# The last norm's turn to token rows: moved into the last product phase, with the deviation applied to rows and eight half-row stores

## What is computed

```python
def odd_block_end(x, mix, l1_w_out_2, final_norm_gain_2):
    x = x + mix @ l1_w_out_2                 # (512, 2048) @ (2048, 2048)
    xf = x.astype(jnp.float32)
    y = xf * lax.rsqrt(jnp.mean(xf * xf, axis=-1, keepdims=True) + 1e-6)
    return y * final_norm_gain_2             # out: (1, 512, 2048)
```

## Time and profile before

| | us |
|---|---|
| median of three executions | 3452.27 |
| lowest, highest | 3450.07, 3458.89 |
| profiled execution | 3455.26 |
| its span in the trace | 3453.5 |
| TensorE busy | 3346.3 (97%) |
| VectorE, ScalarE, GpSimd busy | 1637.2, 1289.0, 520.9 |

### The profile page before, as it was taken

One profiled execution on the slowest core, in us unless ns is written; L12 is line 12 of the kernel. 1 busy time (PEld: TensorE's weight loads), 2 busy tenths in 40 slices (PEclk: granted clock), 3 DMA queues, 4 the chain that ended last, 5 costly groups with the idle time before them and its releaser, 6 DMA issues.

```text
span 3453.5 us, 41721 instructions
## 1 busy us (share of the span) xinstructions
PE 3346.3 (97%) x16417; PEld 2702.4 (78%) x16417; DVE 1637.2 (47%) x2691; ACT 1289.0 (37%) x1997; POOL 520.9 (15%) x754
## 2 busy tenths in 40 slices
PE   7999999999999999999999899999999999999996
PEld 6777887888888888888887676788878788777885
DVE  7895654434344444344344655543324333455532
ACT  4443433343233333433342445433223333456322
POOL 0001312323110000100331010121000111110211
PEclk9999999999999999999999999999999999999998
DMA  6776433546348776544335343453434733433631
GB/s 208 217 234 195 129 104 111 157 141 215 121 169 218 220 216 171 183 146 145 119 108 177 107 132 105 143 193 119 146 85 130 217 120 107 138 116 107 215 129 68
DMA packets 278948, 525.06 MB, mean 152 GB/s; under 512 B 64126, under 2 KB 99525, under 8 KB 273633
## 3 DMA queue, kind: packets, MB, share of 16 engines
q1 hardware_dynamic: 222352, 336.59, 32.6%
q0 software_dynamic: 54224, 182.52, 15.5%
q10 hardware_dynamic: 2176, 3.28, 0.4%
HBM read 408.32 MB, written 113.97 MB: 151 GB/s over the span
## 4 chain that ended last, share of the span: by engine, by line
PE 70%; DVE 4%; ACT 3%; DMA 2%; issue 2%; POOL 1%; ACTq 0%; DVEq 0%; POOLq 0%
PE pg L603 61%; PE pm L1288 2%; PE pm L1317 2%; DMA mx_g<-zt 2%; PE pm L1304 1%; PE pm L2392 1%; ACT whi L386 1%; PE pm L2396 0%; PE pm L2380 0%; DVE r_y L1673 0%; DVE d_x L2480 0%; ACT stage L481 0%; DVE xa L699 0%; ACT w_p L1353 0%; POOL mx_o L850 0%
## 5 line engine op out<-in xcount | busy, mean ns | idle before, releaser
L392 DVE TENSOR_TENSOR wlo<-raw,whi 128x1024 fp32r<-128x1024 f32 x523 | 664.3, 1275 | 1253.9 <-ACT whi L386 1253.0
L386 ACT ACTIVATE whi<-raw 128x1024 fp32r<-128x1024 f32 x523 | 548.6, 1054 | 1103.7 <-PE pg L603 1103.2
L603 PE MATMUL pg<-a_hi,whi 128*128 128x512 f32 x1856 | 744.3, 401 | 11.6 <-DVE wlo L392 4.3
L603 PE MATMUL pg<-a_hi,wlo 128*128 128x512 f32 x1856 | 727.2, 392 | 0.0
L603 PE MATMUL pg<-a_lo,whi 128*128 128x512 f32 x1856 | 726.4, 391 | 0.0
L603 PE MATMUL pg<-b_hi,whi 128*128 128x512 f32 x1568 | 618.9, 395 | 8.9 <-DVE stage L546 3.2
L603 PE MATMUL pg<-b_hi,wlo 128*128 128x512 f32 x1568 | 611.5, 390 | 0.0
L603 PE MATMUL pg<-b_lo,whi 128*128 128x512 f32 x1568 | 611.0, 390 | 0.0
L603 PEld LDWEIGHTS pg<-a_hi,whi 128*128 128x128 f32 x1856 | 348.5, 188 | 91.0 <-issue 14.3
L603 PEld LDWEIGHTS pg<-a_hi,wlo 128*128 128x128 f32 x1856 | 348.3, 188 | 77.9
L603 PEld LDWEIGHTS pg<-a_lo,whi 128*128 128x128 f32 x1856 | 348.9, 188 | 73.6 <-issue 2.6
(11 more groups left out here) (434 smaller groups left out, 3844.8 us busy)
## 6 DMA issues: line engine op xcount, KB each, us to landing
raw<-in_l_w_in SPq DMA_DIRECT2D x169, 512.0 KB, 3.7
raw<-in_ab_w_in SPq DMA_DIRECT2D x112, 512.0 KB, 3.7
zt<-stage POOLq DMA_DIRECT2D x142, 256.0 KB, 3.6
raw<-in_c_w_in SPq DMA_DIRECT2D x64, 512.0 KB, 5.0
raw<-in_l_w_out SPq DMA_DIRECT2D x64, 512.0 KB, 3.7
raw<-in_ab_w_out SPq DMA_DIRECT2D x32, 512.0 KB, 3.7
raw<-in_glu_w SPq DMA_DIRECT2D x32, 512.0 KB, 4.4
raw<-in_c_w_out SPq DMA_DIRECT2D x32, 512.0 KB, 3.7
```

The costliest lines, as they stand in the source:

```text
L386: nc.scalar.activation(used(whi, n), used(raw, n), ACT.Copy).then_inc(hi_ready, 1)
L392: nc.vector.tensor_tensor(used(wlo, n), used(raw, n), used(whi, n).bitcast(F32), ALU.subtract).then_inc(lo_ready, 1)
L603: ins = nc.tensor.matmul(pg[m][:r.rows(m), :r.cols()], lhsT, rhs, start=(kt == 0 and n_pass == 0), stop=(kt == r.kts - 1 and n_pass == 2))
```

## The change

The turning to rows no longer waits for the deviation. A row's deviation is one number per token, so it can be applied after the turn, as a factor per partition.

- In `act_piece` each residual tile of the last phase is also multiplied by its gain into one of four slots (`WEIGHT_SLOTS`: two of `xa_n`, `xa_acc`, `xa_r`), right behind its square.
- `token_rows_pe` transposes the four squares of such a tile into one bank of `pm0` to `pm2`; `token_rows_dve` copies the bank back over the tile in `xa`. For tiles 0 to 11 that is done inside the second to fourth block: the group of tile 4(i-1)+q-2 stands between the two halves of piece q (2 to 5) on TensorE, the copy at piece q+1 on VectorE.
- GpSimd adds 15 squares. The 16th goes to the sum directly: `finish_pe` sums per 128 tokens into one column each, from `acc` and from `xa_sq`, so that the sum stands as tokens by partition (`rstd_col`). Tile 15 is transposed behind the sums.
- The table for Ln and Exp is loaded once, in the second block at piece 2.
- `finish_act` and `finish_dve` multiply the rows of 128 tokens by their deviation into `y_tok`, half a row (1024 features) each; `y_tok` lies over `b_hi` and `b_lo`, so both wait for the last product. `finish_sp` issues eight stores of 512 KB on SyncE's queue and waits for them.

```diff
+    Y = overlay(HALF, [("y_tok", [NTOK, D], F32)])
+    TURNED = 4 * NTOK + 1
+    WEIGHTED = 5 * KT
+    WEIGHT_SLOTS = [XA["xa_n"][:, 0, :], XA["xa_n"][:, 1, :], XA["xa_acc"][:, :], XA["xa_r"][:, :]]
...
+    def token_rows_pe(pe, n):
+        pe.wait_ge(nh_ready, WEIGHTED + n + 1)
+        if n >= 3:
+            pe.wait_ge(xt_ev, TURNED + n - 2)
+        for t in range(NTOK):
+            ins = nc.tensor.transpose(pm[n % 3][:, t * P:(t + 1) * P], WEIGHT_SLOTS[n % 4][:, t * P:(t + 1) * P], ident[:, :])
+        ins.then_inc(xt_ready, 1)
+    def token_rows_dve(dve, n):
+        dve.wait_ge(xt_ready, TURNED + n + 1)
+        nc.vector.tensor_copy(XA["xa"][:, n, :], pm[n % 3][:, :]).then_inc(xt_ev, 1)
     def act_piece(act, r, i, q, extra, part):
         if part == 0:
...
         if extra["joint"] is not None and r is extra["first"] and i == 0 and q == 2:
+        if extra["last"] and i == 1 and q == 2:
+            nc.scalar.preload_act_table_set(LOG_EXP)
         if extra["gain"] is not None and i == r.blocks - 1 and 0 < q < r.pieces - 1:
             for kt in (2 * q - 2, 2 * q - 1):
...
                 if extra["gain"] is not None and i == r.blocks - 1:
+                if extra["last"]:
+                    if n >= 4:
+                        act.wait_ge(xt_ready, TURNED + n - 3)
+                    nc.scalar.activation(WEIGHT_SLOTS[n % 4], x[:, n, :], ACT.Copy, scale=col("last_g", n)).then_inc(nh_ready, 1)
         elif r.evac == "glu":
             for m in range(r.banks):
...
+        if extra["last"] and i and 3 <= q <= 6:
+            token_rows_dve(dve, MT * (i - 1) + q - 3)
         if extra["gain"] is not None and i == r.blocks - 1 and q > 1:
             for kt in (2 * q - 4, 2 * q - 3):
...
+        if extra["last"] and i and part == 1 and 2 <= q <= 5:
+            token_rows_pe(pe, MT * (i - 1) + q - 2)
         if joint is not None and r is extra["first"] and i == 0 and part == 0:
             if q == 3:
...
         elif r.evac == "resid":
             _, _, sq, sq_gained = X_OF["B" if extra["src"] == "A" else "A"]
             sums = [(acc, sq)] + ([(XA["xa_acc"], sq_gained)] if extra["two"] else [])
-            for m in range(r.banks):
+            for m in range(r.banks - 1 if extra["last"] and i == r.blocks - 1 else r.banks):
                 for s, (total, squares) in enumerate(sums):
...
-    def rstd_pe(pe):
-        pe.wait_ge(acc_done, 6 * KT)
-        nc.tensor.matmul(pm[0][:, :], ones[:, :], acc[:, :], start=True, stop=True).then_inc(rs_ready, 1)
-    def rstd_act(act):
+    def finish_pe(pe):
+        for n in range(KT - MT, KT - 1):
+            token_rows_pe(pe, n)
+        pe.wait_ge(acc_done, 6 * KT - 1)
+        pe.wait_ge(sq_ready, 5 * KT)
+        for t in range(NTOK):
+            nc.tensor.matmul(pm[3][:, t:t + 1], acc[:, t * P:(t + 1) * P], ones[:, 0:1], start=True, stop=False)
+            ins = nc.tensor.matmul(pm[3][:, t:t + 1], XA["xa_sq"][:, (KT - 1) % 2, t * P:(t + 1) * P], ones[:, 0:1], start=False, stop=True)
+        ins.then_inc(rs_ready, 1)
+        token_rows_pe(pe, KT - 1)
+    def rows_of_half(t, h):
+        return (Y["y_tok"][:, t, h * D // 2:(h + 1) * D // 2].rearrange("p (k c) -> p k c", c=P),
+                XA["xa"][:, h * KT // 2:(h + 1) * KT // 2, t * P:(t + 1) * P])
+    def finish_act(act):
-        serial(act, act_seq)(nc.scalar.activation(rstd[:, :], pm[0][:, :], ACT.Ln, scale=1.0 / D, bias=eps[:, 0:1]))
-        nc.scalar.activation(rstd[:, :], rstd[:, :], ACT.Exp, scale=-0.5).then_inc(sd_ready, 1)
-    def rstd_dve(dve):
+        serial(act, act_seq)(nc.scalar.activation(rstd_col[:, :], pm[3][:, :NTOK], ACT.Ln, scale=1.0 / D, bias=eps[:, 0:1]))
+        nc.scalar.activation(rstd_col[:, :], rstd_col[:, :], ACT.Exp, scale=-0.5).then_inc(sd_ready, 1)
+        act.wait_ge(sd_ready, 9)
+        act.wait_ge(w_used, pieces_in_all)
+        act.wait_ge(xt_ev, TURNED + KT // 2)
+        for t in range(NTOK):
+            y, x = rows_of_half(t, 0)
+            nc.scalar.activation(y, x, ACT.Copy, scale=rstd_col[:, t:t + 1]).then_inc(nh_ready, 1)
+    def finish_dve(dve):
+        for n in range(KT - MT, KT):
+            token_rows_dve(dve, n)
+        dve.wait_ge(w_used, pieces_in_all)
+        dve.wait_ge(xt_ev, TURNED + KT)
+        for t in range(NTOK):
+            y, x = rows_of_half(t, 1)
+            nc.vector.tensor_scalar(y, x, rstd_col[:, t:t + 1], None, ALU.mult).then_inc(xn_ready, 1)
+    rows_out = ident_in
+    def finish_sp(sp):
+        for t in range(NTOK):
+            for h, (signal, n) in enumerate(((nh_ready, WEIGHTED + KT), (xn_ready, 2 * KT))):
+                sp.wait_ge(signal, n + t + 1)
+                half_row = slice(h * D // 2, (h + 1) * D // 2)
+                sp.dma_start(out[0, t * P:(t + 1) * P, half_row], Y["y_tok"][:, t, half_row]).then_inc(rows_out, 16)
+        sp.wait_ge(rows_out, 16 + 16 * 2 * NTOK)
     def split_norm_dve(dve, x, xn, gain, hi, lo):
```

More of the change, by code:

```diff
@@ L173, in build @@
     r_sp = sb("r_sp", [6, RB])
-    ident_in = sem("identity_in")
+    ident_in = sem("identity_in_and_rows_out")
     NCONST = len(VECTORS) + 3
@@ L695, in split_norm_act @@
             nc.scalar.activation(hi[:, kt, :], xn[:, kt % 2, :], ACT.Copy).then_inc(nh_ready, 1)
[L697 to L700, removed]
     tokens_moved = [sem(f"token_rows_moved{n}") for n in range(NTOK)]
@@ L779, in turn_in_dve @@
         run(vec.tensor_copy(rstd[:, :], pm[0][:, :]))
[L782 to L806, removed]
     def store_x(pool, x, n):
@@ L2559, in details @@
     def details(n):
-        d = dict(ready=None, old=None, acc0=0, xin0=0, gain=None, done=0, two=False, joint=JOINTS.get(n))
+        d = dict(last=(n == L1_OUT), ready=None, old=None, acc0=0, xin0=0, gain=None, done=0, two=False, joint=JOINTS.get(n))
         d.update(DETAILS.get(n, {}))
@@ L2639, in _ @@
             in_turn(products(sp, n, sp_piece))
+        finish_sp(sp)
     @block.gpsimd
@@ L2665, in _ @@
         mixed(mix_pool(pool, 2, ZT["mgate"], L1_GATES, 1), rest, pool, pool_piece, L1_OUT)
-        turn_out_pool(pool, XB["xb_tok"])
     @block.tensor
@@ L2689, in _ @@
         mixed(mix_pe(pe), rest, pe, pe_piece, L1_OUT)
-        rstd_pe(pe)
-        turn_out_pe(pe, XA["xa"])
+        finish_pe(pe)
     @block.scalar
@@ L2718, in _ @@
         mixed(mix_act(act, 2), rest, act, act_piece, L1_OUT)
-        rstd_act(act)
-        turn_out_act(act, XB["xb_tok"])
+        finish_act(act)
     @block.vector
@@ L2752, in _ @@
         mixed(mix_dve(dve, 2, B["b_lo"]), rest, dve, dve_piece, L1_OUT)
-        rstd_dve(dve)
-        scale_x_dve(dve, XA["xa"], "last_g")
+        finish_dve(dve)
     ctx.close()
```

## The result

| | before | after |
|---|---|---|
| median, us | 3452.26 (4 executions) | 3432.66 (4 executions) |
| lowest, highest | 3450.07, 3458.89 | 3431.25, 3434.74 |
| profiled execution | 3455.26 | 3432.28 |
| its span | 3453.5 | 3430.5 |

The ratio is 0.9943, with an interval of 0.9931 to 0.9955: the change takes off 0.57%, 19.6 us, where 19.2 was forecast.

The account below looks back on a forecast made before the run. TensorE bounds the kernel up to the last matmul, then a chain no product covers. Earlier last landing -19.1, transposes among the products +5.7, shorter landing to end -5.8: -19.2, so 3433.1 us; range 3427 to 3440.

Follow-up runs that it names:

- the version with mixed stores: The version with all transposes behind, but with five stores: first 128 rows in two halves, the other three groups whole (1 MB); 3427.05 us, ratio 0.9931.
- the version with all transposes behind: Changed kernel with all sixteen transpose groups behind the last product, none inside the product phase; 3427.16 us, ratio 0.9930; measured again 3427.77, 0.9929.

## What to carry to other kernels

Issue the last stores from an engine whose drain is short, and let GpSimd finish early: here that was 6 of the 19.6 us, for one changed queue. Once the end is bound by the stores, only the way to the first store and the bytes count; work that can run beside the transfer belongs there and not in a phase that TensorE fills. To compare two traces, measure both from the same event near the change: the spans differed by 3.5 us more than the kernels did.

## What the hardware showed that I had not expected

- An issue of a store on SyncE's queue takes 0.36 us at first and, in the kernel after, 1.19 or more from the fourth of the eight on, at no cost here, since nothing waits behind it. Full DMA engines alone don't make it so: the five stores of the version with mixed stores took 0.33 to 0.36 each, though the last three were issued with the engines full (415 GB/s).
- GpSimd's drain takes 5.6 to 6.2 us behind whatever the engine did last, an add as well as a wait for a DMA. SyncE's takes 7 ns behind its stores, and 124 in the earlier trace rows.
- Eight stores of 512 KB with rows of 4 KB moved at 405 GB/s from SyncE's queue and 392 from GpSimd's, four of 1 MB with rows of 8 KB at 421 from SyncE's.
- A second group of four transposes right behind a first costs 0.425 us, the first 0.485.
- With TensorE busy but for 0.28 us ahead of the sums, the granted clock fell to half behind the sums in one of the three traces of the version with all transposes behind, and not in the other two.
- The clock also rose while TensorE did nothing but transposes: in the kernel before, whose 64 transposes begin at 3428.97 behind 13.4 us without work, it was 0.50 from 3429 to 3434 and 1.00 from 3434.8 to 3440.
